# The MLP's second product by pairs of units as seven half-size products in place of eight

## The reference

```python
h = rmsnorm_2(x, norm_mlp_w[l]) * (1.0 + sc2) + sh2
ff = jnp.square(jax.nn.relu(h @ mlp_w1[l])) @ mlp_w2[l]
x = x + g2 * ff
return rmsnorm_2(x, final_norm_w)
```

## Time and profile before

| | us |
|---|---|
| median of 3 runs | 1253.55 (1253.31 to 1256.31) |
| the profiled execution | 1254.99, its span 1253.2 |
| PE busy | 1234.6 |
| DVE busy | 702.9 |
| ACT busy | 671.5 |
| POOL busy | 370.4 |

### The profile page before, as it was taken

How to read it: one execution, slowest core, us unless ns; L and a number is a source line. 1 busy time by engine, 2 the same in 40 slices (tenths; PEclk the granted TensorE clock), 3 DMA queues, 4 the chain that set the end, 5 groups by cost and what they waited for, 6 DMA issues and landing times.

```text
span 1253.2 us, 19051 instructions
## 1 busy us (share of the span) xinstructions
PE 1234.6 (99%) x7098; PEld 992.7 (79%) x7098; DVE 702.9 (56%) x1486; ACT 671.5 (54%) x1278; POOL 370.4 (30%) x191
## 2 busy tenths in 40 slices
PE   9999999999999999899999999999999999999998
PEld 8777777778877777688776887888988888888887
DVE  6776667775576666475798545684762121221223
ACT  6666666675437676635667885753542232231331
POOL 0000000004310000054486874123355344353451
PEclk9999999999999999999999999999999999999999
DMA  5322254334242332254132021341363233233232
GB/s 204 110 65 85 85 168 127 126 119 134 85 118 77 101 93 85 68 185 117 44 100 70 19 78 58 117 135 55 98 218 118 71 114 101 84 109 93 84 101 67
DMA packets 38410, 128.10 MB, mean 102 GB/s; under 512 B 4640, under 2 KB 7584, under 8 KB 38320
## 3 DMA queue, kind: packets, MB, share of 16 engines
q1 hardware_dynamic: 35792, 121.91, 31.4%
q10 hardware_dynamic: 2528, 4.98, 1.3%
HBM read 123.43 MB, written 2.13 MB: 100 GB/s over the span
## 4 chain that ended last, share of the span: by engine, by line
PE 80%; ACT 7%; DVE 6%; issue 5%; DMA 1%; POOL 1%; ACTq 0%; DVEq 0%; SPq 0%; POOLq 0%
PE G L868 20%; PE G L870 19%; PE G L869 19%; ACT scr L1249 2%; PE S L995 2%; PE O L1056 2%; PE S L1707 1%; DVE wL L2455 1%; PE T L1035 1%; ACT wH L1952 1%; PE S L1725 1%; DMA w<-weights_dram 1%; POOL tmp L533 1%; PE G L840 1%; PE G L841 1%
## 5 line engine op out<-in xcount | busy, mean ns | idle before, releaser
L498 POOL TENSOR_TENSOR wL<-w,wH 128x1024 fp32r<-128x1024 f32 x119 | 290.4, 2445 | 825.2 <-ACT wH L1952 825.2
L868 PE MATMUL G<-hi,wH 128*128 128x512 f32 x1208 | 487.3, 403 | 0.4 <-DVE xT L963 0.4
L870 PE MATMUL G<-hi,wL 128*128 128x512 f32 x1208 | 472.4, 391 | 0.0
L869 PE MATMUL G<-lo,wH 128*128 128x512 f32 x1208 | 472.0, 391 | 0.0
L868 PEld LDWEIGHTS G<-hi,wH 128*128 128x128 f32 x1208 | 227.6, 188 | 56.1 <-issue 9.9
L1952 ACT ACTIVATE wH<-w 128x1024 fp32r<-128x1024 f32 x170 | 179.1, 1054 | 168.1 <-PE G L870 112.5
L870 PEld LDWEIGHTS G<-hi,wL 128*128 128x128 f32 x1208 | 227.3, 188 | 49.3
L869 PEld LDWEIGHTS G<-lo,wH 128*128 128x128 f32 x1208 | 228.0, 189 | 45.1 <-issue 1.5
L965 DVE SCALAR_TENSOR_TENSOR xT<-G,modT,xT 128x512 f32<-128x512 f32 x34 | 25.5, 751 | 124.1 <-PE G L870 124.0
L2455 DVE TENSOR_TENSOR wL<-w,wH 128x1024 fp32r<-128x1024 f32 x51 | 62.3, 1221 | 42.7 <-ACT wH L1952 41.9
L2427 ACT ACTIVATE tmp<-G 128x512 f32<-128x512 f32 x31 | 18.5, 597 | 120.1 <-PE G L870 116.8
(11 more groups left out here) (461 smaller groups left out, 1903.2 us busy)
## 6 DMA issues: line engine op xcount, KB each, us to landing
w<-weights_dram SPq DMA_DIRECT2D x170, 512.0 KB, 3.6
adaw<-ada_dram SPq DMA_DIRECT2D x43, 512.0 KB, 4.2
kd<-c_dram ACTq DMA_DIRECT2D x8, 512.0 KB, 3.8
cbias<-ada_dram SPq DMA_DIRECT2D x5, 512.0 KB, 4.4
xT<-x_dram SPq DMA_DIRECT2D x4, 512.0 KB, 8.0
out_dram<-xT SPq DMA_DIRECT2D x8, 256.0 KB, 2.2
scr<-ca_dram SPq DMA_DIRECT2D x2, 512.0 KB, 4.9
kd<-cbias SPq DMA_DIRECT2D x8, 128.0 KB, 4.1
```

The lines of the kernel that those rows point to most:

```text
L498: g.tensor_tensor(wL[:, u.slot], w32[:, u.slot % 2], wH[:, u.slot].bitcast(f32), ALU.subtract).then_inc(w_lo, 1)
L868: mm(home[:, :], whi, H[:, k, :], start=(k == first), stop=False)
L869: mm(home[:, :], whi, L[:, k, :], start=False, stop=False)
L870: last = mm(home[:, :], wlo, H[:, k, :], start=False, stop=(k == final))
```

## The change

The first product stays as it was, but its hidden features come in another order (tile n/2 of the contraction's first half for even n, of its second half for odd n). Of the second product's 32 units 30 are now done as 15 pairs; the last two stay plain.

A pair is 256 output features (two units) by 1024 of contraction, seen as 2 x 2 blocks A11, A12, A21, A22 of 128 x 512 (rows: unit, columns: half of the contraction). The activations are 2 x 2 blocks too: halves of the contraction by halves of the tokens. The product of 2 x 2 by 2 x 2 blocks is formed with seven block products in place of eight (Winograd's form of Strassen's): A11, S1, S2, S4, A12, S3 and A22 name the weight side, where S1 = A21 + A22, S2 = S1 - A11, S3 = A11 - A21, S4 = A12 - S2. Each meets a token half or one of four sums of them. A product is 4 tiles x 3 matmuls of 256 columns; some go on adding to a bank that a former one has left.

What is new on each engine:

- PE (`product`, `first_tiles`): 84 matmuls of 256 columns for a pair in place of 48 of 512. The order of the products is written out; between two products of a pair stand products of the next. `PLACE` is that order.
- DVE: for a pair the weight sums S1, S2, S4 (512 columns, S1 of two operands in SBUF, results in the PSUM banks O and N) and their low parts, and seven additions `take` of 256 columns in place of two of 512. In the first product the four sums of token halves for each pair of units.
- ACT: seven high parts of 512 columns for a pair (`high_of`), in place of two of 1024; high parts of the token sums.
- POOL: the sum S3, the low parts of A11, A12, S3, A22, and those of the token sums.
- SP: `load_pair` brings a pair, 2 x 512 KB, by turns into a new home `wp` and into both slots of `w32`. A pair waits for the last use of the pair before the last; the next quarter's first units wait until the fourth pair in `w32` is used up.

The pieces, high and low, have a ring of 10 places (`PIECES`), seven per pair. Tiles of earlier stages now share memory with the new ones. The loop over quarters 1 and 2 is written out.

```diff
+A11, S1, S2, S4, A12, S3, A22 = range(7)
+
+PLACE = [[0, 1, 3, 4, 5, 7, 10], [2, 6, 8, 9, 11, 12, 15], [13, 14, 16, 17, 18, 19, 22], [20, 21, 23, 24, 25, 26, 27]]
...
+def multiplied(q, i):
+
+    c, p = divmod(q, 4)
+    return 28 * c + (20 if (q, i) == (PAIRS - 1, A22) else PLACE[p][i]) + 1
...
+        def pair_home(q):
+            return w32 if q % 2 else wp
+
+        def piece(q, i):
+            return (7 * q + i) % PIECES
...
+            def load_pair(q):
+                if q > 1:
+                    sp.wait_ge(*mark("piece_sum", 3 * (q - 2) + 3))
+                    sp.wait_ge(*mark("piece_lo_g", 4 * (q - 2) + 4))
+                for n in range(2):
+                    sp.dma_start(pair_home(q)[:, n], a["weights"][UM + 34 + 2 * q + n].rearrange("p (k n) -> p k n", k=KT)
+                                 ).then_inc(pair_here[q % 2], 16)
 
...
+                        load_ada(Block(ADA_M, n - 3))
+                if c == 0:
+                    sp.wait_ge(*mark("lo_mlp", 16))
+                load_pair(4 * c)
+                if c == 0:
+                    for n in range(5, 8):
+                        load_ada(Block(ADA_M, n))
+                sp.wait_ge(w_lo, UM + 8 * c + 8)
+                load_pair(4 * c + 1)
+                load_pair(4 * c + 2)
+                if c < 3:
+                    load_pair(4 * c + 3)
+                sp.wait_ge(*mark("piece_sum", 3 * (4 * c + 3 - 2 * (c == 3)) + 3))
+                sp.wait_ge(*mark("piece_lo_g", 4 * (4 * c + 3 - 2 * (c == 3)) + 4))
+                for n in range(5 if c < 3 else 2):
+                    load_unit(Unit(UM + 8 * c + 8 + n))
...
+            def low_of(q, i, home):
+                pool.wait_ge(*mark("piece_hi", 7 * q + i + 1))
+                g.tensor_tensor(pieceL[:, piece(q, i)], home, pieceH[:, piece(q, i)].bitcast(f32), ALU.subtract).then_inc(piece_lo_g, 1)
+
+            def third_sum(q):
+                raw = pair_home(q)
+                pool.wait_ge(*mark(f"pair_here{q % 2}", 32 * (q // 2) + 32))
+                wait(pool, *mark("piece_lo_g", 4 * q - 1))
+                g.tensor_tensor(third, raw[:, 0, 0:4], raw[:, 1, 0:4], ALU.subtract).then_inc(piece_third, 1)
+
+            def sum_low(c, k, x, n=1):
+                pool.wait_ge(*mark("f_sum_hi", 3 * (4 * c + k) + x))
+                low = sum_home(c, x, k, True) if n == 1 else sumL[:, x - 2:x - 2 + n, k, :]
+                high = sum_home(c, x, k) if n == 1 else sumH[:, x - 2:x - 2 + n, k, :]
+                g.tensor_tensor(low, raw_sum[:, x - 1, :] if n == 1 else raw_sum[:, x - 1:x - 1 + n, :], high.bitcast(f32),
+                                ALU.subtract).then_inc(f_sum_lo, 1)
+
+            def pieces(q):
+                low_of(q, A11, pair_home(q)[:, 0, 0:4])
+                third_sum(q)
+                low_of(q, A12, pair_home(q)[:, 0, 4:8])
+                low_of(q, S3, third)
+                low_of(q, A22, pair_home(q)[:, 1, 4:8])
+
+            def quarter(c):
+                q = 4 * c
+                for n in range(8):
+                    if n % 2 == 0:
+                        sum_low(c, n // 2, 1)
+                    else:
+                        sum_low(c, n // 2, 2)
+                        sum_low(c, n // 2, 3, 2)
+                    if n < 5:
+                        split_lo(Unit(UM + 8 * c + 3 + n))
+                    if n == 5:
+                        low_of(q, A11, pair_home(q)[:, 0, 0:4])
+                        third_sum(q)
+                    if n == 6:
+                        low_of(q, A12, pair_home(q)[:, 0, 4:8])
+                    if n == 7:
+                        low_of(q, S3, third)
+                        low_of(q, A22, pair_home(q)[:, 1, 4:8])
+                for p in range(2 if c == 3 else 3):
+                    pieces(q + p + 1)
+                for n in range(2 if c == 3 else 3):
+                    split_lo(Unit(UM + 8 * c + 8 + n))
+            for c in range(4):
+                quarter(c)
             g.wait_ge(*mark("end_root", 1))
             for k in range(2):
...
+            def product(q, i, home, moving, first, tiles=range(4)):
+
+                at = piece(q, i)
+                for k in tiles:
+                    high, low = moving(k)
+                    mm(home, pieceH[:, at, k, :], high, start=first and k == 0, stop=False, skip_group_check=True)
+                    mm(home, pieceH[:, at, k, :], low, start=False, stop=False, skip_group_check=True)
+                    last = mm(home, pieceL[:, at, k, :], high, start=False, stop=(k == 3), skip_group_check=True)
+                if tiles[-1] == 3:
+                    last.then_inc(product_done, 1)
...
+            def product_1(q):
+                c, p = divmod(q, 4)
+                pe.wait_ge(*mark("piece_lo_g", 4 * q + 1))
+                if p < 2:
+                    pe.wait_ge(sem("f_sq"), 8 * c + 7 + p)
+                else:
+                    pe.wait_ge(*mark("x_part", multiplied(q - 2, A22)))
+                pe.wait_ge(sem("f_lo"), 8 * c + 7)
+                product(q, A11, G[p % 2][:, HALF[0]], tokens(0, 0), True)
+
...
+            def first_tiles(c):
+                q = 4 * c
+                product_1(q)
+                product_5(q)
+                product_1(q + 1)
+                product_6(q, range(3))
+                product_3(q, range(3))
+                product_6(q, range(3, 4))
+                product_3(q, range(3, 4))
+                product_2(q)
+                product_5(q + 1)
+                product_7(q)
+                product_6(q + 1)
+                product_3(q + 1)
+                product_4(q)
+                product_2(q + 1)
+                product_7(q + 1)
+                product_1(q + 2)
+                product_5(q + 2)
+                product_4(q + 1)
+                product_6(q + 2)
+                product_3(q + 2)
+                product_2(q + 2)
+                product_7(q + 2)
+
...
+                if c == 3:
+                    return
+                product_1(q + 3)
+                product_5(q + 3)
+                product_4(q + 2)
+                product_6(q + 3)
+                product_3(q + 3)
+                product_2(q + 3)
+                product_7(q + 3)
+                gemm(pe, Unit(UM + 8 * c + 8), hi2, lo2, mark("x_part", multiplied(q + 2, A22)), part=FIRST)
+                product_4(q + 3)
+                gemm(pe, Unit(UM + 8 * c + 8), hi2, lo2, None, part=SECOND)
+                gemm(pe, Unit(UM + 8 * c + 9), hi2, lo2, mark("x_part", multiplied(q + 3, A22)))
...
+            def high_of(q, i, home):
+                if 7 * q + i >= PIECES:
+                    act.wait_ge(*mark("product_done", multiplied(*divmod(7 * q + i - PIECES, 7))))
+                s.activation(pieceH[:, piece(q, i)], home, ACT.Copy).then_inc(piece_hi, 1)
...
+            def pieces(q):
+                raw_high(q, A11)
+                sum_high(q, S1)
+                sum_high(q, S2)
+                sum_high(q, S4)
+                raw_high(q, A12)
+                third_high(q)
+                raw_high(q, A22)
...
+            def quarter(c):
+                q = 4 * c
+                for n in range(8):
+                    k = n // 2
+                    act.wait_ge(gemm_done, UM + 8 * c + n + 1)
+                    wait(act, sem("f_sq"), 8 * c + n)
+                    s.activation(relu[:, :], (N if c == 0 and n == 2 else G[n % 2])[:, :], ACT.Relu).then_inc(sem("f_relu"), 1)
+                    if n % 2:
+                        act.wait_ge(*mark("f_sum", 4 * (4 * c + k) + 2))
+                        s.activation(sum_home(c, 2, k), raw_sum[:, 1, :], ACT.Copy).then_inc(sem("f_sum_hi"), 1)
+                        act.wait_ge(*mark("f_sum", 4 * (4 * c + k) + 4))
+                        s.activation(hi1[:, 4 + k, :], T[1][:, :], ACT.Copy).then_inc(sem("f_hi"), 1)
+                        s.activation(sumH[:, 1:3, k, :], raw_sum[:, 2:4, :], ACT.Copy).then_inc(sem("f_sum_hi"), 1)
+                    else:
+                        act.wait_ge(*mark("f_sum", 4 * (4 * c + k) + 1))
+                        if c == 3:
+                            s.activation(hi1[:, k, TWO], later_half[:, :], ACT.Copy)
+                        s.activation(hi1[:, k, HALF[0]], T[0][:, HALF[0]], ACT.Copy).then_inc(sem("f_hi"), 1)
+                        s.activation(sum_home(c, 1, k), raw_sum[:, 0, :], ACT.Copy).then_inc(sem("f_sum_hi"), 1)
+                    if n < 5:
+                        split_hi(Unit(UM + 8 * c + 3 + n))
+                    if n == 5:
+                        raw_high(q, A11)
+                        sum_high(q, S1)
+                    if n == 6:
+                        sum_high(q, S2)
+                        sum_high(q, S4)
+                        raw_high(q, A12)
+                    if n == 7:
+                        third_high(q)
+                        raw_high(q, A22)
+                pieces(q + 1)
+                if c == 3:
```

(78 more changed lines are left out.)

346 lines of the change are left out of this document (244 added, 102 removed).

## The result

| | before | after |
|---|---|---|
| median, us | 1254.33 (1253.31 to 1256.31) | 1302.95 (1302.85 to 1304.92) |
| profiled execution, its span | 1254.99, 1253.2 | 1303.05, 1301.3 |
| ratio after/before | | 1.0396 (95%: 1.0383 to 1.0410) |
| PE busy, matmuls | 1234.6, 7098 | 1237.2, 7638 |

The changed kernel is 4.0% slower, 48.6 us between the medians of this table. 1287 was forecast, 33.5 us more than before, with a range of 1270 to 1302: the direction and the places were as forecast, the sum was 16 us short, and the time lies just outside of the range.

The account below looks back on a forecast made before the run. PE (TensorE) was taken as the limit of each MLP stage; -12.0 saved, +28.3 border 1, +10.8 border 2, +6.4 clock gave +33.5 us on 1254.99, 1288.5, stated as a median of 1287, range 1270 to 1302.

Parts of the forecast that it names:

- the term for the clock: PE's granted clock falls at each border 1, 1.6 us four times, 6.4 us; bounds 0 and 12.
- border 1: First to second product, each quarter: PE waits for POOL's low part of second pair's A11; 28.3 us in all, bounds 22 and 32.
- the rest zero: Kernel's end, last half units and moved squares cost zero, -0.5 to +1.5; written-out loops -0.5 to +0.5.
- Price of PE's work: Second product: seven products of 256-column matmuls, 0.120 us each, save 0.80 us a pair, 12.0 us for fifteen pairs.
- rival (f): Half-size matmuls cost 0.130 us in a long run, so the 12.0 gain goes: 1299; chance within main case's 62.
- Border 2: Second product back to next quarter's first: PE waits 3.6 us for a late unit load, three times, 10.8; bounds 0 and 15.
- (a): The gain arrives: border 1 vanishes with the clock's fall, border 2 hidden; 1241, range 1240 to 1250; 8 in 100.
- (b): Only border 1: the quarter's end hides, so 1287 - 10.8 = 1276; 12 in 100.
- (c): Only the waits at the borders, no fall of the clock: 1281; 15 in 100, within the main case's 62.
- (d): A border costs little, POOL's and DVE's lists turning out short by 2 us each: 1255 to 1270; 7 in 100.
- (e): Followers turn late: mid-quarter slack of 1.6 us is missing, 15 pairs each wait 1 us: 1302; 11 in 100.

Follow-up runs that it names:

- the best orders of the lists: Kernel with first pair's pieces one unit earlier, plus next unit loaded into `wp` and two POOL splits moved: 1254.96 us; also with quarter 0's first pair loaded earlier: 1252.89 us.
- the last order of the lists: The 1254.96 us kernel (early pieces, next unit in `wp`) with quarter 0's first pair loaded before unit 5: 1252.89 us, ratio 0.9988.

## Where the prediction was right and where it failed

The time came out above the range. The step that failed is the term for the clock, one fall of 1.6 us at each border 1, 6.4 in all, where the runs show 15.1; border 1's own length (28.3 against 33.1) and "the rest zero" (3.8) follow. That is 17.3 us too little, of which the profiled execution's early start of the MLP (2.5 us, below) hides a part. That the direction and the places were right isn't luck: the waits are the ones named.

- **Price of PE's work: right.** 12.0 forecast, 12.4 measured, since the 1213 matmuls of 256 columns that start at full rate are 0.1197 us apart in the mean. So rival (f), that they cost more in a long run, is out. Every new wait of PE is paid in full, as forecast.
- **Border 1: the mechanism right, the term short by 4.8.** 28.3 forecast, 33.1 measured (9.5 / 10.2, 6.2 / 7.4, 6.2 / 7.4, 6.4 / 8.1). The released operation is the one named. What was mis-sized is the pace of DVE and POOL, for which the sum took rows in which each works alone, while this change puts them side by side. The forecast named the rule of the Trainium skill (SBUF — State Buffer, Who interferes with whom), estimated 0.7 us for each border and left it out of the sum. Without such a sum the time lost is 6.0 us in quarters 1 and 2, against the forecast's 6.2; with it 7.4. The rule was right and worth twice the estimate, for the forecast looked only at the one sum of the second pair beside POOL's list of the border. The first pair's sum in unit 5 meets POOL too, and it is worth more (0.98 against 0.46).
- **Border 2: right.** 10.8 forecast, 10.8 measured (3.57 + 3.69 + 3.54 from start to start).
- **The clock: right in kind, and the step that failed.** 6.4 forecast, 15.1 measured. I counted one fall of 1.6 us at each border 1. In the rows the half rate costs 2.1, 2.1, 2.1 and 1.9 us there, 8.2; and it also came after each border 2, 1.4 + 1.6 + 1.4 = 4.4, which I had put into the bound alone; 2.5 more is in the first matmuls after each halt, in those in which the clock changes, and in a wait of 0.26 us in quarter 0. The bound of 12 was too low as well: the price was taken from a stretch of 3.4 us, while here matmuls start at half rate for 4.3 to 4.9 us after the standstill of border 1.
- **"The rest zero": wrong by 3.8.** Before quarter 0's unit 3 (1.29), before its first product (1.05, DVE's low part) and before the last half units (1.02, POOL's split) PE waits. The first shows how such a step fails:

```profile
904.31 1.82 POOL L646 TENSOR_TENSOR lo<-sq,hi 128x256 fp32r<-128x256 f32 x1 [14.27 <-ACT hi L2715]
...
906.09 2.37 POOL L572 TENSOR_TENSOR wL<-w,wH 128x1024 fp32r<-128x1024 f32 x1
...
908.51 0.50 PE L987 MATMUL G<-hi,wH 128*128 128x512 f32 x1 [1.29 <-POOL wL L572]
```

  A small new operation stands ahead of a split that PE needs; where the lists have no lead yet, at the start of the MLP, it is not hidden. I had checked the bulk of each unit's list, not the start and the end.

- **The rivals.** (a), the gain arrives: not in this kernel; the best orders of the lists, 1254.96 and 1252.89, don't reach its 1240 to 1250 either. (b), border 1 alone, and (c), no fall of the clock: refuted by the waits and by the half-rate rows. (d), small borders: refuted in the changed kernel; with one product moved border 1 is 3.0 us in quarters 1 and 2. (e), late followers: no product in mid-quarter waits; its 1302 is close to the result by chance.

The terms together, with PE's work at the prices of the account: -12.0 + 33.1 + 10.8 + 3.8 + 15.1 = +50.8, less the 0.2 that was there before, +50.6 for 50.5 measured. The profile of the changed kernel reached the MLP 2.5 us earlier than the one of before (901.6 against 904.1; it was 901.6 to 905.5 in all these executions), which gives the 48.1 by which the spans differ. Part of that variation is the clock: ahead of the MLP it fell at 728.6 and 773.0 in the profile before and only at 815.8 in the one after. Whether the change itself moves this part isn't shown.

What stays open: whether quarter 0 could lose its last 5.0 us of halts with the `ada` blocks done elsewhere, and what the last order of the lists would take with the sum's second operand in PSUM; neither was tried.

## What to carry to other kernels

A change that takes work off the limiting engine by giving much more to the others is decided by the order of their lists: carry each list through the borders of a stage, and ask of every operation that the limiting engine needs what stands ahead of it. Here 12 us of saved products stood against 44 us of waits that no busy share shows, and moving one product or one load won back 18 and 11 us. Price each wait of TensorE with the clock that it loses besides, and price operations of VectorE and GpSimd by rows in which they meet.
